# Down products of both FFNs: 16 of 22 contraction tiles as seven block products of 256 tokens

## The reference

```
def swiglu(x, w_gate, w_up, w_down):
    return (jax.nn.silu(x @ w_gate) * (x @ w_up)) @ w_down

u = rmsnorm(h, ffn1_pre_norm)
h = h + 0.5 * rmsnorm(swiglu(u, w_gate, w_up, w_down), ffn1_post_norm)
```

## Time and profile before

| | us |
|---|---|
| median of three runs | 1182.58 |
| lowest and highest | 1180.94, 1183.28 |
| the profiled execution | 1181.91 |
| span of its profile | 1180.0 |
| TensorE busy in it | 1168.5 |
| VectorE busy | 817.1 |
| ScalarE busy | 582.9 |
| GpSimd busy | 131.0 |

### The profile page before, as it was taken

How to read it: one execution, slowest core, us unless ns; L and a number is a source line. 1 busy time by engine, 2 the same in 40 slices (tenths; PEclk the granted TensorE clock), 3 DMA queues, 4 the chain that set the end, 5 groups by cost and what they waited for, 6 DMA issues and landing times.

```text
span 1180.0 us, 17769 instructions
## 1 busy us (share of the span) xinstructions
PE 1168.5 (99%) x6860; PEld 1008.6 (85%) x6860; DVE 817.1 (69%) x1309; ACT 582.9 (49%) x921; POOL 131.0 (11%) x111
## 2 busy tenths in 40 slices
PE   9999999999999999999999999999999999999997
PEld 8899999988888886667887888789999998888886
DVE  6898888773337787665467775688888886333674
ACT  6555555532236527566333623575555554322573
POOL 7000000000014000001012201340000000000344
PEclk9999999999999999999999999999999999999999
DMA  6233333332331331111522233232333334233211
GB/s 217 80 107 107 107 107 107 121 128 90 103 86 36 91 107 53 37 37 38 159 90 72 73 108 114 85 96 79 107 107 107 99 103 148 95 92 104 90 36 72
DMA packets 101854, 111.99 MB, mean 95 GB/s; under 512 B 15294, under 2 KB 91678, under 8 KB 101542
## 3 DMA queue, kind: packets, MB, share of 16 engines
q1 hardware_dynamic: 97542, 109.18, 29.8%
q10 hardware_dynamic: 4256, 2.12, 0.6%
HBM read 108.12 MB, written 3.16 MB: 94 GB/s over the span
## 4 chain that ended last, share of the span: by engine, by line
PE 91%; DVE 4%; ACT 2%; issue 2%; POOL 0%; ACTq 0%; DVEq 0%; POOLq 0%
PE bank L303 14%; PE bank L305 14%; PE bank L304 14%; PE bank L781 10%; PE bank L782 10%; PE bank L783 10%; PE bank L626 2%; PE bank L620 2%; PE bank L621 2%; PE bank L310 1%; PE bank L311 1%; PE bank L312 1%; PE bank L1369 1%; PE bank L455 1%; PE bank L1348 1%
## 5 line engine op out<-in xcount | busy, mean ns | idle before, releaser
L337 DVE TENSOR_TENSOR w_lo<-w_raw,w_hi 128x1024 fp32r<-128x1024 f32 x121 | 155.8, 1297 | 173.6 <-ACT w_hi L330 173.3
L330 ACT ACTIVATE w_hi<-w_raw 128x1024 fp32r<-128x1024 f32 x121 | 125.8, 1054 | 191.9 <-PE bank L305 183.1
L782 PE MATMUL bank<-T_lo,w_hi 128*128 128x256 f32 x576 | 163.1, 283 | 0.0
L781 PE MATMUL bank<-T_hi,w_hi 128*128 128x256 f32 x576 | 163.1, 283 | 0.0
L783 PE MATMUL bank<-T_hi,w_lo 128*128 128x256 f32 x576 | 163.1, 283 | 0.0
L303 PE MATMUL bank<-T_hi,w_hi 128*128 128x512 f32 x352 | 137.4, 390 | 0.0
L304 PE MATMUL bank<-T_lo,w_hi 128*128 128x512 f32 x352 | 137.0, 389 | 0.0
L305 PE MATMUL bank<-T_hi,w_lo 128*128 128x512 f32 x352 | 137.0, 389 | 0.0
L303 PE MATMUL bank<-v_hi,w_hi 128*128 128x512 f32 x328 | 132.8, 405 | 0.0
L305 PE MATMUL bank<-v_hi,w_lo 128*128 128x512 f32 x328 | 128.3, 391 | 0.0
L304 PE MATMUL bank<-v_lo,w_hi 128*128 128x512 f32 x328 | 127.9, 390 | 0.0
(11 more groups left out here) (311 smaller groups left out, 2329.8 us busy)
## 6 DMA issues: line engine op xcount, KB each, us to landing
w_raw<-in_ffn_w_up SPq DMA_DIRECT2D x44, 512.0 KB, 4.1
w_raw<-in_ffn_w_down SPq DMA_DIRECT2D x44, 512.0 KB, 3.5
w_raw<-in_ffn_w_gate SPq DMA_DIRECT2D x43, 512.0 KB, 4.3
w_raw<-in_w_in SPq DMA_DIRECT2D x32, 512.0 KB, 3.6
w_raw<-in_w_out SPq DMA_DIRECT2D x8, 512.0 KB, 3.3
w_raw<-in_ple_w_gate SPq DMA_DIRECT2D x8, 512.0 KB, 3.4
x_tm<-in_x SPq DMA_DIRECT2D x4, 512.0 KB, 6.9
Mb<-m_rows ACTq DMA_DIRECT2D x8, 256.0 KB, 4.9
```

Of the source, the lines that this page charges most:

```text
L330: nc.scalar.activation(w_hi[:, s, :], w_raw[:, s, :], ACT.Copy).then_inc(w_hi_done, 1)
L337: nc.vector.tensor_tensor(w_lo[:, s, :], w_raw[:, s, :], w_hi[:, s, :].bitcast(F32), ALU.subtract).then_inc(w_lo_done, 1)
L781: nc.tensor.matmul(o, whi, a_hi(kk), start=(start and kk == 0), stop=False, skip_group_check=True)
L782: nc.tensor.matmul(o, whi, a_lo(kk), start=False, stop=False, skip_group_check=True)
```

## The change

In each FFN, the contraction tiles 0 to 15 of the down product become one block product. Weights, inputs and outputs are halved: contraction 0 to 7 and 8 to 15, output tiles 0 to 3 (lower) and 4 to 7 (upper), tokens 0 to 255 (left) and 256 to 511 (right). Seven products take four chunks each, a chunk holding two contraction tiles by 512 outputs. Chunks are now 28 + 6 for each down stage instead of 22.

The chunks of products 0, 1 and 6 are plain blocks loaded into `w_raw`. Those of products 2 to 5 are sums of blocks, and no engine computes them: SyncE loads a block into `sum_a` (which lies over v_hi) or `sum_b` (over v_lo), and GpSimd issues DMA transfers that add another block from HBM onto it (`accum_op=ALU.add`), four for each of four groups. Each waits until the value before has been split. The differences of `prod` are made by VectorE (`down_raw_dve`) into `wsum` or `scratch`. Between products, ScalarE copies halves of banks (`down_copy_act`) and VectorE adds them (`down_seed_dve`). Four matmuls of 512 tokens write the upper banks once so that later ones add to them. The lower output comes out with its sign turned: for the six tiles left, the weights of the lower half are negated when they are split, and the gain of the norm behind is negated for them.

```diff
+            def down_product(p, left, upper, first=False):
+                a_hi, a_lo = down_operand(T_hi, p), down_operand(T_lo, p)
+                for c in range(4):
+                    nw = DN + 4 * p + c
+                    pe.wait_ge(w_lo_done, nw + 1)
+                    if c % 2 == 0:
+                        own.wait(pe, "t_lo", 4 + 2 * p + c // 2 + 1)
+                    for m in range(4):
+                        if first and c == 2 and m == 3:
+                            own.wait(pe, "post", POST1)
+                            for u in range(4, 8):
+                                nc.tensor.matmul(B[YBANK[u]][:], wv(nw, 0, P)[0], a_hi[:, 0:2, :].rearrange("p k c -> p (k c)"),
+                                                 start=True, stop=True)
+                        if c == 0:
+                            if p == 0 and m == 0:
+                                own.wait(pe, "post", POST1 - 4)
+                            if p == 1:
+                                own.wait(pe, "rcopy", COPY0 + m + 1)
+                            if p == 3:
+                                own.wait(pe, "rcopy", COPY0 + 4 + m + 1)
+                            if p == 4:
+                                own.wait(pe, "post", POST1 + m + 1)
+                            if p == 6:
+                                own.wait(pe, "post", POST1 + 4 + m + 1)
...
+                        for kk in range(2):
+                            k = 2 * c + kk
...
+                            nc.tensor.matmul(o, whi, a_hi[:, k, :], start=start, stop=False, skip_group_check=True)
+                            nc.tensor.matmul(o, whi, a_lo[:, k, :], start=False, stop=False, skip_group_check=True)
+                            last = nc.tensor.matmul(o, wlo, a_hi[:, k, :], start=False, stop=(k == 7), skip_group_check=True)
```

SyncE's loads and GpSimd's adding transfers:

```diff
+            for c in range(4):
+                rows_loaded(DN + c, 2 * c, 0, None)
+            own.wait(sp, "mm", 7 * (QUADS - 1) + 6)
+            for c in range(4):
+                sp.dma_start(sum_a[:, c, :, :], block_rows(2 * c, 1)).then_inc(part_in[c], 16)
+            for c in range(4):
+                rows_loaded(DN + 4 + c, SK // 2 + 2 * c, 0, DN + c)
+            own.wait(sp, "mm", MM0)
+            for c in range(4):
+                sp.wait_ge(w_loaded[(DN + 4 + c) % RING], LOADED[DN + 4 + c])
+                sp.dma_start(sum_b[:, c, :, :], block_rows(2 * c, 0)).then_inc(consts_in, 16)
+            for c in range(4):
+                rows_loaded(DN + 24 + c, SK // 2 + 2 * c, 1, DN + 8 + c)
...
+            for c in range(4):
+                pool.wait_ge(part_in[c], 16 + 16 * (n // 2) + 16)
+                pool.wait_ge(w_hi_done, DN + 4 + c + 1)
+                pool.dma_start(sum_a[:, c, :, :], block_rows(SK // 2 + 2 * c, 1), accum_op=ALU.add).then_inc(own[f"sum{c}"], 16)
+            for c in range(4):
+                pool.wait_ge(w_lo_done, DN + 8 + c + 1)
+                pool.dma_start(sum_a[:, c, :, :], block_rows(2 * c, 0), accum_op=ALU.add).then_inc(own[f"sum{c}"], 16)
+            pool.wait_ge(consts_in, CONSTS + 64 * (n // 2) + 64)
+            for c in range(4):
+                own.wait(pool, f"sum{c}", 32)
+                pool.dma_start(sum_b[:, c, :, :], block_rows(2 * c, 1), accum_op=ALU.add).then_inc(own[f"sum{c}"], 16)
+            for c in range(4):
+                own.wait(pool, f"sum{c}", 48)
+                pool.wait_ge(w_lo_done, DN + 12 + c + 1)
+                pool.dma_start(sum_a[:, c, :, :], block_rows(SK // 2 + 2 * c, 0), accum_op=ALU.add).then_inc(own[f"sum{c}"], 16)
```

The order of work on VectorE and on ScalarE (a slot is one chunk of one product):

```diff
+            raws = {(0, 1): (2, 0), (0, 3): (2, 1), (1, 3): (3, 0), (2, 0): (3, 1), (2, 1): (4, 0), (2, 3): (4, 1),
+                    (3, 1): (6, 0), (4, 1): (6, 1)}
+            for p in range(7):
+                for c in range(4):
+                    if (p, c) in raws:
+                        down_raw_dve(dve, *raws[p, c])
+                    if p < 6 and c in (0, 2):
+                        down_lo_dve(dve, p + 1, c // 2)
...
+                    if c == 3 and p in (3, 4):
+                        for m in range(4):
+                            down_seed_dve(dve, p, m)
+                    lo_upto(dve, DN + 4 * p + 4 + c)
...
+            for p in range(7):
+                for c in range(4):
+                    if p < 6 and c in (0, 2):
+                        down_hi_act(act, p + 1, c // 2)
...
+                    if c == 3 and p in (0, 2, 4):
+                        for m in range(4):
+                            down_copy_act(act, p, m)
+                    hi_upto(act, DN + 4 * p + 4 + c)
```

More of the change, by code:

```diff
@@ L732, in split_slot, with product_done, down_operand, block_rows @@
         def split_slot(tile, k):
-            s = k % 4
+            s = (k - SK + 4) % 8
             return tile[:, s // 2, 2 * (s % 2):2 * (s % 2) + 2, :].rearrange("p a c -> p (a c)")
+        def product_done(eng, p, m):
+            if m < 3:
+                own.wait(eng, "mm", MM0 + 3 * p + m + 1)
+            else:
+                eng.wait_ge(w_used, DN + 4 * p + 4)
+        def down_operand(tile, p):
+            return tile[:, 2 * (p % 2):2 * (p % 2) + 2, :, :].rearrange("p a k c -> p (a k) c")
+        def block_rows(k0, row):
+            c = 512 * (1 - row)
+            return wd[0, k0 * P:(k0 + 2) * P, c:c + 512].rearrange("(k p) c -> p k c", p=P)
+        for c in range(4):
+            chunk = lambda t: t[:, c, :, :].rearrange("p k c -> p (k c)")
+            for e in range(4):
+                src = chunk(sum_b if e == 2 else sum_a)
+                summed[DN + 8 + 4 * e + c] = (src, own[f"sum{c}"], own.before(f"sum{c}") + 16 * (e + 1))
         def sp_load(sp, i, j):
@@ L760, in sp_prog, with rows_loaded @@
                     sp_load(sp, i, j)
[L761 to L764, removed]
+            def rows_loaded(n, k0, row, then):
+                if n < DN + 4:
+                    qd = QUADS - 2 + (n - DN) // 2
                     own.wait(sp, "s_dve", 4 * qd + 4)
@@ L839, in down @@
+            down_product(0, False, False, first=True)
+            down_product(1, True, True)
+            down_product(2, True, False)
+            down_product(3, False, False)
+            down_product(4, False, False)
+            down_product(5, False, True)
+            down_product(6, True, False)
+            for j in range(4):
+                pe.wait_ge(w_lo_done, CONVENTIONAL + j + 1)
+                own.wait(pe, "t_lo", 18 + j + 1)
                 for m in range(KD):
-                    if first and m in (0, 4):
-                        own.wait(pe, "post", POST0 + 4 * (QUADS - 1 + m // 4))
@@ new lines, in down_seed_dve @@
+        def down_seed_dve(dve, p, m):
+            right = B[YBANK[m]][:, 256:512]
+            if p == 3:
+                own.wait(dve, "rcopy", COPY0 + 4 + m + 1)
+                product_done(dve, p, m)
+                nc.vector.tensor_tensor(B[YBANK[m + 4]][:, 256:512], right, r5_down[:, m, :], ALU.add).then_inc(own["post"], 1)
+            else:
+                own.wait(dve, "rcopy", COPY0 + 8 + m + 1)
+                nc.vector.tensor_tensor(right, right, r5_down[:, m, :], ALU.add).then_inc(own["post"], 1)
```

203 lines of the change are left out of this document (145 added, 58 removed).

## The result

| | median us | lowest, highest | runs | mean granted clock of the profiled run |
|---|---|---|---|---|
| before, on the same chip | 1182.7 | 1180.94, 1183.28 | 4 | 0.997 |
| after | 1192.78 | 1190.52, 1199.8 | 4 | 0.985 |

The ratio is 1.0094, with a 95% interval from 1.0071 to 1.0116. So the change made the kernel slower by 0.9%, where 1174.4 us, a gain, had been forecast; the time lies inside the stated range, by 0.2 us, but moved the other way. The profiled execution of after is the longest of its four (1199.8 us, span 1197.7 us); the other three lie between 1190.52 and 1193.83 us.

The account below looks back on a forecast made before the run. The down stage was taken as bound by its matmuls. Per FFN: -5.62 matmuls, +0.24 start, +0.3 product 1, +0.2 product 4, +0.8 transfer stall = -4.08 us; both -8.2, so 1174.4 us, range 1171.0 to 1193.0 us.

Parts of the forecast that it names:

- What bounds the kernel: Down stage: bound by number and width of matmuls; VectorE, ScalarE and DMA have room, DMA busy a third of the time.
- rivals 1 and 2: GpSimd's additions: two passes, 1188.0 us, chance 0.22; or three passes or one by one, 1217.8 us, chance 0.10.
- Part 1: Block products' matmuls: 672 of 256 tokens at 0.120 us replace 384 of 512 tokens, -5.62 us in each FFN.
- S: Stall from late additions, the larger of the delays at products 3 and 4: forecast 0.8 us per FFN.
- Rival 4: Written-out short matmuls not supplied at 0.120 us: at 0.130 us, 13.4 us more, 1187.8 us, chance 0.05.
- Part 2: Start of the down stage: an old stall of 0.21 us goes, a later start adds 0.45 us; net +0.24 us.
- Part 3: Splitting on ScalarE and VectorE: both fit, nearly full; waits of +0.3 us at product 1 and +0.2 us at product 4.
- the walk: First FFN's transfers added in order from 235.9 us, giving when chunks and additions land before products 1, 3 and 4.
- Part 4: Transfers of the down stage, said to decide the case: 16 loads and 16 additions in the first 70 us; stall 0.8 us.
- a: DMA engine time of one 512 KB addition onto SBUF: taken as 2.04 us, between 1.36 and 4.08 us.
- rival 1: Additions take two passes, 2.72 us each, and transfers become the bound: stall 7.6 us, 1188.0 us, chance 0.22.
- the milder form of rival 1: An addition takes between 2.25 and 2.47 us of the DMA engines: 1179 to 1183 us, chance 0.16.

Follow-up runs that it names:

- plain-load kernel: The changed kernel with all sixteen GpSimd transfers of each FFN loading instead of adding (sums left out): 1175.38 us, ratio to before 0.9939.
- the last kernel of the experiments: The changed kernel with product 6's loads later and product 2's copies, product 3's seeds and the first tile's low part earlier: 1175.41 us, ratio to before 0.9941.
- the copies first: The changed kernel with only ScalarE's four copies behind product 2 moved ahead of w_hi of DN+14: 1190.69 us, ratio to before 1.0079.
- the late sum_b: The changed kernel with the loads of product 6 and the four loads into sum_b both issued later: 1189.2 us, ratio to before 1.006.

## Why the prediction was wrong

**What bounds the kernel: right for before.** The room seen in the earlier trace rows was real, but on the DMA engines the change spent more than there was: their share from 236 to 303 us is 1.05, the "near 1" that the prediction gave as the sign of rivals 1 and 2.

**Part 1, the matmuls: right.** The written-out products step at 0.120 us, as the earlier trace rows has it for the loop, and the four bank-writing matmuls add 0.81 us (0.93 us between starts less the step), for 0.91. Rival 4 (not supplied in time) is refuted. The plain-load kernel is 7.1 us faster than before, both FFNs together, where the sum gives -9.8 without S; its measured gaps (0.42 us at each start, 0.66 and 1.62 us at product 1, 0.26 us at each product 4) make it -8.0, and the rest was not pinned down.

**Part 2, the start: right.** 0.54 us between the last step of the loop and the first of the down stage, so +0.42 us for 0.45.

**Part 3: right in its causes, product 1 too cheap in the second FFN.** The wait at product 1 is 0.46 us in the first FFN (0.3 priced, 0 to 1.5), and 1.78 us in the second, outside the bounds. The rows of PE, ScalarE and VectorE in after:

```profile
251.22 0.36 PE L934 MATMUL bank<-T_hi,w_hi 128*128 128x256 f32 x1 [0.30 <-DVE w_lo L362]
250.72 1.18 ACT L1126 ACTIVATE bank<-bank 128x256 f32<-128x256 f32 x4
249.99 1.22 DVE L362 TENSOR_TENSOR w_lo<-w_raw,w_hi 128x1024 fp32r<-128x1024 f32 x1
```

PE's row names w_lo, but this w_lo (249.99 to 251.21) is that of DN+5, and product 1 begins with DN+4, whose w_lo started at 247.71; PE's weight load, at 251.19, even starts before it ends. What product 1 does wait for are the copies (`rcopy`), as predicted: PE starts 0.50 us after the first one, 0.51 in the second FFN, and the same 0.51 stands between the copies and product 3. The copies came later than priced because the loads ahead of them did: w_hi of DN+4 starts at 246.62 where the walk had its chunk landed at 244.8, and in the second FFN another 1.3 us later, counted from the loop's end. The seeds wait of product 4 is 0.26 us for 0.2.

**Part 4, the term that failed.** "I take the middle between one pass and two, a = 2.04 us": it measured 2.54 us, near the two passes (2.72) of rival 1. The middle had no row behind it, only that reading SBUF may go partly beside the read of HBM; the time of an addition, 1.87 times that of a load, leaves little room for that. The Trainium skill's ratio of 1.93 for a reducing transfer (Collectives: The Full Stack, "The bandwidth ceiling: the fold count and why AG ≠ RS ≠ AR") was the better guide: the 1.87 measured here agrees with it, for an addition into SBUF outside any collective.

But a alone does not give the result. With 2.54 us the prediction's own walk says product 3 late by 7 x 2.54 - 13.5 = 4.3 us and product 4 by 11 x 2.54 - 22.3 = 5.6, so S = 5.6, +0.8 us for each FFN and 1184.1 us, against the 1182.58 us of before that its rivals are counted from: that term alone turns the forecast's gain into none. (By the same formula the milder form of rival 1 gives 1177.7 to 1182.6 us, not 1179 to 1183.) Measured were 7.62 us at product 3 and only 0.26 us at product 4: the wait that decided was that for the seventh addition, not the eleventh. What the walk lacked:
- One more plain transfer. It counted three loads of product 6 ahead of the seventh addition; the spacing of 3.95 us shows one beside each of four additions: +1.4 us.
- The rest of the way to the seventh addition, which lands at 280.4, for 238.0 + 20.4 + 17.8 = 276.2 by the walk at a = 2.54: +2.8 us more. From 238 to 280.4 us the engines moved 290 GB/s, 12.3 MB, which is the 16 loads and 7.4 additions. So about 1.1 us went into additions behind the seventh that were under way beside it, where the walk has them one after the other. The other 1.7 us were not assigned. The plain loads by themselves are not their cause as a whole: from 238 to 242 us they moved 334 GB/s, less than the 386 of the walk, but from 242 to 250 us 396.
- **The clock behind the gap, which the prediction did not look for.** 27 steps in 5.82 us where 3.24 would do: +2.6 us in the first FFN, and +2.5 in the second. A stall was priced at its own length, and this one cost a third more.

The account of the first FFN: -5.62 (matmuls) - 0.21 (old stall gone) + 0.42 (start) + 0.46 (product 1) + 7.62 (product 3) + 2.58 (clock) + 0.26 (product 4) = +5.5 us. From the last step of the gate and up loop to the start of the stage's last matmul it is 126.75 us after and 121.00 before, +5.75 us. For the second FFN, with 1.78 at product 1, 0.31 within product 2, 7.96 at product 3, 2.49 by the clock and again 0.26 at product 4, the same sum gives +7.4 us, against 128.71 - 121.02 = +7.7 in the traces. The profiled spans differ by 17.7 us, so 4.3 us lie outside the two down stages: 0.7 ahead of the first, 0.3 between them and 3.3 behind the second; see what stays open. In the three shorter runs of after the mean clock was 0.989 to 0.991 instead of 0.985, so the loss by the clock is smaller in them than in this account.

So the step that failed is a of part 4, and beside it the clock, a term put at nothing; what happened was rival 1, with its mechanism: ScalarE takes its waits in order, and the transfers become the bound. Its 1188.0 us were too low although its a was too high, by the clock and the items above. That its S of 7.6 us equals the 7.62 measured is luck: it was worked out for the eleventh addition and product 4, and for product 3 its a gives 7 x 2.72 - 13.5 = 5.5 us. Its 0.22 and the milder form's 0.16 were too little: the one argument against it was about rates of HBM, and nothing in the trace spoke for a second read being free. The other side of the forecast was not wrong in size: the last kernel of the experiments, with four pieces moved, comes to -7.5 us against before, where -8.2 had been forecast (and it no longer pays the start, 0.84 us of that sum).

**What stays open.** In the profiles of after and of some experiments the clock is also at half for some 4 to 6 us after the second FFN (after: 0.50 from 1124 to 1130 us), in others and in before it is not; behind the first FFN the clock dips in before too (mean 0.84 from 357 to 368 us). Beside it goes the scatter within one kernel: of the six runs of the last version the two at a mean clock of 0.998 took 1173.7 and 1173.8 us, the two at 0.994 took 1177.5 and 1178.8. What sets this off there was not found; PE has no long gap ahead of it. Nor were the two parts of a long gap's cost, the wait and the clock, tried apart. And the cost by the clock does not follow the length of the gap alone, as the figures below show.

## What to carry to other kernels

A transfer that adds into SBUF is no load: price it at about 1.9 times a plain one of the same size, 2.54 us for 512 KB with all engines, and add up every transfer that has to land before a given instruction, those of later stages that SyncE has put among them too. Move loads that are wanted late out of the crowded stretch first (12.8 us here, more than any change of order on an engine), then put the short instructions that PE waits for (copies out of banks, seeds) ahead of pieces that wait for a transfer on their engine, one after the other, since the next takes the place of the last.

## What the runs showed of the hardware

- An adding transfer takes more of its issuer too: 1.20 us of GpSimd for each issue, against 0.72 us for the same transfer as a plain load. GpSimd's timeline in after, then its group in the plain-load kernel:

```profile
285.98 1.20 POOL L1347 DMA_DIRECT2D sum_a<-in_ffn_w_down  x1 [1.32 <-DMA sum_b<-in_ffn_w_down]
```

```profile
L1343 POOL DMA_DIRECT2D sum_b<-in_ffn_w_down x4 | 2.9, 722 | 3.8 <-DMA sum_a<-in_ffn_w_down 3.8
```

- A gap on PE is paid twice when it is long. What the slow steps behind it cost beyond 0.12 us each: 2.5 to 2.6 us behind the four gaps of 7.4 to 8.2 us of after (both measurements), 1.5 and 2.0 us behind the 7.83 and 7.69 us of the kernel with the last two groups plain, 2.7 us behind the 5.20 us of the copies first, 1.6 us behind the three gaps of 3.8 to 4.6 us (the late sum_b, the copies first), and nothing behind those up to 2.2 us, where the clock stayed at 1.00. Behind the three of 3.8 to 4.6 us PE began at full steps and fell to the slow ones only after 6 to 11 of them, so the fall came when PE was at work again. Shortening the gap by 5.5 us took 7.7 us off the first FFN's down stage.
- The DMA share of the windows goes to 1.13 with additions alone in flight and to 1.02 with plain loads: a share near or over 1 says that the engines are full, and only the GB/s beside it (206 against 388) what that fullness is worth.
- The releaser in a row of PE can be an instruction that merely ended at the same time: at product 1 it is w_lo of a chunk not yet wanted, and the copies are what was waited for. The program's order of waits decides between them.
